# Gate stage of a PEER layer: eight tokens per set of tiles instead of four, two tokens innermost, and every low part of that stage on VectorE

## The chip, the core and the metric

The kernel runs on one core of one Trainium2 chip. The metric is the device time of one execution in microseconds (us); below, PE is TensorE, DVE is VectorE, ACT is ScalarE, POOL is GpSimd and SP the engine that issues the transfers from memory. PEld is TensorE's loading of stationary operands, which overlaps its matmuls.

## The reference, cut to what matters

Two blocks of a model are computed for 256 tokens of width 1024. The change lies in the PEER layer of the first block, which has 16384 experts, numbered by two indices of 128 each. Per token, 128 (expert, gate) pairs are selected:

```python
idx = jnp.take_along_axis(cidx, pos, axis=-1)      # cidx = i1 * 128 + i2
gates = jax.nn.softmax(best, axis=-1)
...
act = jax.nn.gelu(jnp.einsum('tkd,td->tk', ue, ht), approximate=False)
ve = jnp.take(v, it, axis=0)
return jnp.einsum('tk,tkd->td', gt * act, ve)
```

The kernel gathers nothing. It computes gelu(h · u) for all 16384 experts and all tokens, multiplies it by a gate that is zero for experts not selected, and multiplies by all of v.

## The kernel before, in words

**Units.** All weights stream through in units of 128x1024 fp32 (512 KB): SP loads unit i into `raw`, ACT writes its rounded high part `whi` (`hi`), and DVE or POOL writes the low part `wlo = raw - whi` (`lo`); `on_pool` decides which of the two by a table, and in the stretch `BASE["u"] + 62 <= slot <= BASE["v"] + 62` it gave every other unit to POOL. PE forms every product from three matmuls (high by high, high by low, low by high; `three`). There are three buffers of `whi` and `wlo`, so `hi` of unit i waits until PE is done with unit i - 3.

**Stages.** The 128 units of `u` are followed by the 128 units of `v`. A unit of u is 24 matmuls of 256 columns, a unit of v is 12 matmuls of 512 columns. ACT's gelu writes the activations `acts`, 128 partitions by 128 (second index) by 256 (tokens); in the views they are tile A. In the v stage ACT and DVE cut each slice of `acts` into a high part (`cut_acts`, into the buffer of hTh) and a low part (hTl), which PE then uses as stationary operands.

**The gate stage.** For each token PE makes the 128 x 64 gates of one half of the second index by three bf16 matmuls (the gate is split into three bf16 parts): stationary is a one-hot of the first index (`oh1`, tile oh), moving is a one-hot of the second index times the gate part (`og`). DVE builds these: `oh` by comparing `iota_b` with `row_b`, `og_eq` by comparing `iota_b` with `col_b`, `og` by multiplying `og_eq` with `gate3`. PE's product lands in a bank of PSUM and DVE multiplies it into `acts` (`weigh`; in the views "A<-A,bank"). Half 0 is done beside the units u+64 to u+127, half 1 beside v+0 to v+61; half 0 must be complete before v begins (ACT's `cut_acts` waits for `g_mul`), half 1 before v+64.

**What sets the order.** Each engine has its own program. After each unit a program calls `side.step()`, which advances the generator `gates(half)` to its next `yield`; `side.drain()` runs it to its end. Before the change one group is OB = 4 tokens, there are 64 groups a half, and one step is one group. DVE builds two groups ahead of what it weighs (two buffers each of `oh1` and `og`). A few steps are doubled (`U2_STEPS`, and n in (20, 40) in the v stage), so that the groups are done two units before the half's end. Before v+62 all programs call `side.drain()`.

Of the kernel before, what the change touches and what calls it, by code (L numbers as in the profile page):

```python
# [16 lines left out]
P = 128  # L17
D = 1024
T = 256
# [7 lines left out]
UNIT = 1024  # L27
NRAW = 4
NSPL = 3
OB = 4  # L30


STREAMS = [
# [80 lines left out]
def on_pool(i):  # L114

    slot = i - 2
    if BASE["u"] <= slot < BASE["u"] + 62:
        return True
    if BASE["u"] + 62 <= slot <= BASE["v"] + 62:
        return i % 2 == 1  # L120
    if BASE["w_xk"] <= slot < BASE["w_xk"] + 6 or BASE["w_up"] <= slot < BASE["w_up"] + 44:
        return i % 2 == 1
    return BASE["w2_t"] + 4 <= slot < BASE["w2_out"] + 8
# [12 lines left out]
UNITS = [(name, i) for name, k in STREAMS for i in range(k)]  # L136
ACC = {name: i + 1 for i, name in enumerate(("w_in_hi", "w_out", "v", "w_xv", "w2_out", "w_xo", "w_down"))}
U1_STEPS = (1,) * 13 + (2,)
U2_STEPS = (1,) * 31 + (2,)

SEMS = """
hi lo_dve lo_pool w acc0 ev_act ev_dve
# [47 lines left out]
def build(nc, x, mem, wdram, keep_d, con0_d, con1_d, con2_d, keys_d, w2c_d, gf_d, gf2_d, out):  # L190
    ctx = ExitStack()
    with ctx:
# [16 lines left out]
            iT = sb("iT", 3 * T, c=c)  # L209
        with ExitStack() as c:  # L210
            wgp = (sb("wgh", 8 * 36, F32R, c), sb("wgl", 8 * 36, F32R, c))
        oh1 = sb("oh1", 2 * OB * P, BF16)
        og_eq = sb("og_eq", OB * 64, BF16)
        og = sb("og", 2 * 3 * OB * 64, BF16)
        gate3 = sb("gate3", 3 * T, BF16)
        row_b = sb("row_b", T, BF16)
        col_b = sb("col_b", T, BF16)
        iota_b = sb("iota_b", P * OB, BF16)

        with ExitStack() as c:  # L220
            A1 = sb("A1", 24576, c=c)
# [21 lines left out]
        def t3(ap, a):  # L243
            return ap.rearrange("p (a b) -> p a b", a=a)
# [150 lines left out]
        def pe_program(e):  # L395
# [199 lines left out]
                yield  # L595

            def gates(half):
                for g in range(T // OB):
                    G = 64 * half + g
                    z = g % 2  # L600
                    o1 = t3(oh1[:, z * OB * P:(z + 1) * OB * P], P)
                    o3 = t4(og[:, z * 3 * OB * 64:(z + 1) * 3 * OB * 64], 3, 64)
                    if g:
                        yield
                    bk = 4 * half + g % 4
                    e.wait_ge(s["g_og"], G + 1)
                    use(bk)
                    for q in range(OB):
                        for j in range(3):
                            ins = mm(banks[bk][:, q * 64:(q + 1) * 64], o1[:, :, q], o3[:, j, :, q], j == 0, j == 2)  # L610
                    ins.then_inc(s["g_pe"], 1)
                    free[bk] = (s["g_mul"], G + 1)
                yield

            def mem_norm():
                for _ in range(4 + 2 + 2):
# [257 lines left out]
            side.drain()  # L874
            lin_T(BASE["u"] + 62, 2, hTv, KD)
            side.lists[0].append(gates(0))
            lin_T(BASE["u"] + 64, 64, hTv, KD, steps=U2_STEPS)
            side.drain()
            side.lists[0].append(gates(1))

# [2 lines left out]
            for n in range(128):  # L883
                if n == 62:
                    side.drain()
                if n == 126:
                    continue
                both = [n] if n < 126 else [126, 127]
                wv = [unit(BASE["v"] + m) for m in both]
                for m in both:  # L890
                    e.wait_ge(s["ca_lo"], m + 1)
                for b in range(TB):
                    for m, w in zip(both, wv):
                        for h in range(2):
                            ins = three(banks[2 * b + h][:, :], [z[:, m % 8, b * P:(b + 1) * P] for z in acth],
                                        [z[:, h * 512:(h + 1) * 512] for z in w], m == 0, m == 127)
                        if b == 1:
                            ins.then_inc(s["w"], 1)
                    if b == 0 and n == 127:
                        ins.then_inc(s["acc0"], 1)  # L900
                side.step(2 if n in (20, 40) else 1)
                if n == 72:
                    side.lists[0].append(mem_norm())
            for i in range(4):
# [67 lines left out]
        def act_program(e):  # L972
# [121 lines left out]
                for _ in range(8):  # L1094
                    yield

            def gates(half):
                for g in range(T // OB):
                    if g:
                        yield  # L1100
                yield

            def cut_acts(n):
                if n > 127:
                    return
                e.wait_ge(s["g_mul"], 64 if n < 64 else 128)
                e.wait_ge(s["w"], BASE["v"] + max(n - 7, 0))
                act(acth[0][:, n % 8, :], acts[:, n, :], ACT.Copy).then_inc(s["ca_hi"], 1)

# [226 lines left out]
            lin_T(BASE["u"], 62, gelu(0), steps=U1_STEPS)  # L1336
            side.drain()
            lin_T(BASE["u"] + 62, 2, gelu(62))
            side.lists[0].append(gates(0))
            lin_T(BASE["u"] + 64, 64, gelu(64), steps=U2_STEPS)  # L1340
            side.drain()
            side.lists[0].append(gates(1))
            cut_acts(0)
            cut_acts(1)
            for n in range(128):
                hi(BASE["v"] + n + 2)
                if n == 62:
                    side.drain()
                cut_acts(n + 2)
                if n == 126:  # L1350
                    continue
                side.step(2 if n in (20, 40) else 1)
                if n == 72:
                    side.lists[0].append(mem_norm())

# [82 lines left out]
        def dve_program(e):  # L1438
# [224 lines left out]
            def routing(b):  # L1663
# [43 lines left out]
                for _ in range(3):  # L1707
# [1 line left out]
                e.wait_ge(s["rt_pe"], b + 1)  # L1709
                e.tensor_copy(t3(iT[:, :], 3)[:, :, b * P:(b + 1) * P], t3(banks[b][:, 0:384], 3)  # L1710
                              ).then_inc(s["rt_dve"], 1)
                gt = iT[:, 2 * T + b * P:2 * T + (b + 1) * P]
                e.wait_ge(s["rt_dve"], 4 * b + 3)
                e.tensor_copy(row_b[:, b * P:(b + 1) * P], iT[:, b * P:(b + 1) * P])
                e.tensor_copy(col_b[:, b * P:(b + 1) * P], iT[:, T + b * P:T + (b + 1) * P])
                for j in range(3):
                    gj = gate3[:, j * T + b * P:j * T + (b + 1) * P]
                    if j < 2:
                        own(e.tensor_copy(gj, gt))
                        again()  # L1720
                        own(tt(gt, gt, gj, ALU.subtract))
                        again()
                    else:
                        e.tensor_copy(gj, gt).then_inc(s["rt_dve"], 1)
                yield

            def gates(half):
                lo64 = 64 * half
                e.wait_ge(s["rt_dve"], 8)

                def weigh(g):
                    G = 64 * half + g
                    t = g * OB
                    pb = banks[4 * half + g % 4]
                    e.wait_ge(s["ev_act"], PAIR_FREED[PAIR["u"] + 31 + 32 * half][1])
                    e.wait_ge(s["g_pe"], G + 1)
                    sl = acts[:, lo64:lo64 + 64, t:t + OB]
                    tt(sl, sl, pb[:, 0:64 * OB].rearrange("p (t i) -> p i t", t=OB), ALU.mult).then_inc(s["g_mul"], 1)

                for g in range(T // OB):  # L1740
                    G = 64 * half + g
                    z, t = g % 2, g * OB
                    o1 = oh1[:, z * OB * P:(z + 1) * OB * P]
                    o3 = og[:, z * 3 * OB * 64:(z + 1) * 3 * OB * 64]
                    if G >= 2:
                        e.wait_ge(s["g_pe"], G - 1)
                    shape = [P, P, OB]
                    tt(t3(o1, P), t3(iota_b[:, :], P), row_b[:, t:t + OB].unsqueeze(1).to_broadcast(shape),
                       ALU.is_equal)
                    shape = [P, 64, OB]  # L1750
                    if G:
                        e.wait_ge(s["g_og"], G)
                    own(tt(t3(og_eq[:, :], 64), t3(iota_b[:, lo64 * OB:(lo64 + 64) * OB], 64),
                           col_b[:, t:t + OB].unsqueeze(1).to_broadcast(shape), ALU.is_equal))
                    shape = [P, 3, 64, OB]
                    again()
                    tt(t4(o3, 3, 64), t3(og_eq[:, :], 64).unsqueeze(1).to_broadcast(shape),
                       t3(gate3[:, :], 3)[:, :, t:t + OB].unsqueeze(2).to_broadcast(shape), ALU.mult
                       ).then_inc(s["g_og"], 1)
                    if g:  # L1760
                        yield
                        weigh(g - 1)
                weigh(T // OB - 1)
                yield

            def cut_acts(n):
                if n > 127:
# [326 lines left out]
                norm_scale(1, xres, scr, b)  # L2094
            for k2 in range(4):
                norm_lo(1, "g_ffn", hTv, k2)
            own(e.tensor_copy(t3(iota_b[:, :], P), K_("iota").unsqueeze(2).to_broadcast([P, P, OB])))
            lin_T(BASE["w_pq"], 16)
            side.lists[0] += [routing(0), routing(1)]
            lin_T(BASE["u"], 62, steps=U1_STEPS)  # L2100
            side.drain()
            lin_T(BASE["u"] + 62, 2)
            side.lists[0].append(gates(0))
            lin_T(BASE["u"] + 64, 64, steps=U2_STEPS)
            side.drain()
            side.lists[0].append(gates(1))
            cut_acts(0)
# [1 line left out]
            for n in range(128):  # L2109
                lo(BASE["v"] + n + 2)  # L2110
                if n == 62:
                    side.drain()
                cut_acts(n + 2)
                if n == 126:
                    continue
                side.step(2 if n in (20, 40) else 1)
                if n == 72:
                    side.lists[0].append(mem_norm())

# [77 lines left out]
        def pool_program(e):  # L2197
# [49 lines left out]
            for n in range(128):  # L2247
                lo(BASE["v"] + n + 2)
                if n == 126:
                    continue  # L2250
                side.step(2 if n in (20, 40) else 1)
                if n == 72:
                    side.lists[0].append(mem_norm())
            rstd(3)
# [219 lines left out]
```

## Time and profile before

| | |
|---|---|
| median of three runs | 1638.8 us (1636.22 to 1640.73) |
| profiled execution, its own time | 1635.05 us |
| its span | 1633.3 us |
| mean granted clock of TensorE | 0.983 of full speed |
| units u+64 to u+127 with half 0 of the gates | about 483 to 717 us of the span |
| units v+0 to v+61 with half 1 of the gates | about 719 to 947 us |

The profiled execution's time is 1.75 us above its span. A time in a view counts from the span's start. A matmul's duration includes the way through the array, so the durations of neighbours overlap; what a matmul costs is the distance from its start to the next start.

### The profile page before, as it was taken

How to read it: one execution, taken by the hardware profiler on the slowest of the kernel's cores; microseconds unless marked ns; L12 is line 12 of the kernel's file. 1: busy time of each engine (PE TensorE's matmuls, PEld its weight loads, DVE VectorE, ACT ScalarE, POOL GpSimd, SP SyncE). 2: the span in 40 equal slices, each digit the busy share in tenths (PEclk: the TensorE clock that was granted, in tenths of full speed). 3: DMA queues.
4: the chain of work that ended last, by engine and by line, in shares of the span. 5: the costliest groups of instructions: out<-in, count | busy, mean ns of one | idle time of the engine just before them, and what ended most of it. 6: DMA issues, size and time to landing. Idle time of an engine off the chain costs nothing.

```text
span 1633.3 us, 26555 instructions
## 1 busy us (share of the span) xinstructions
PE 1521.8 (93%) x10784; PEld 1370.5 (84%) x10784; DVE 1142.6 (70%) x1894; ACT 719.4 (44%) x1031; POOL 488.5 (30%) x222
## 2 busy tenths in 40 slices
PE   7989989999999999999999999999886889898897
PEld 7979879989999999987777888888874668788876
DVE  4564653958838888879999966555689654577754
ACT  4762544444443333333333345445451544444443
POOL 4000000898963333333332300000353440133310
PEclk9999999999999999999999999999997899999999
DMA  6433454455554444444444466555322233444453
GB/s 219 132 127 106 142 175 160 164 161 180 168 181 143 142 143 140 146 134 151 141 144 142 142 237 215 183 191 168 130 95 73 82 128 113 142 155 155 155 183 114
DMA packets 66937, 245.15 MB, mean 150 GB/s; under 512 B 7424, under 2 KB 7552, under 8 KB 66560
## 3 DMA queue, kind: packets, MB, share of 16 engines
q1 hardware_dynamic: 66816, 243.45, 45.3%
q8 instruction: 86, 1.41, 0.4%
q14 instruction: 35, 0.29, 0.1%
HBM read 242.37 MB, written 1.05 MB: 149 GB/s over the span
## 4 chain that ended last, share of the span: by engine, by line
PE 70%; DVE 16%; ACT 7%; POOL 4%; issue 3%; DMA 0%; DVEq 0%; ACTq 0%; SPq 0%; POOLq 0%
PE bank L406 70%; DVE A L1448 4%; DVE A L1455 4%; ACT whi L978 4%; POOL wlo L2205 3%; DVE A L1452 2%; ACT A L978 2%; DVE wlo L1452 1%; PE bank L415 1%; DVE A L1449 1%; DVE A L1978 0%; ACT L978 0%; POOL small L2211 0%; DVE A L1991 0%; DVE xres L1452 0%
## 5 line engine op out<-in xcount | busy, mean ns | idle before, releaser
L978 ACT ACTIVATE whi<-raw 128x1024 fp32r<-128x1024 f32 x448 | 472.0, 1056 | 465.4 <-PE bank L406 464.0
L2205 POOL TENSOR_TENSOR wlo<-raw,whi 128x1024 fp32r<-128x1024 f32 x179 | 458.4, 2567 | 580.9 <-ACT whi L978 579.8
L406 PE MATMUL bank<-hTh,whi 128*128 128x256 f32 x1944 | 562.8, 290 | 30.2 <-DVE wlo L1452 16.4
L406 PE MATMUL bank<-hTh,wlo 128*128 128x256 f32 x1944 | 549.9, 283 | 0.0
L406 PE MATMUL bank<-hTl,whi 128*128 128x256 f32 x1944 | 549.5, 283 | 0.0
L1452 DVE TENSOR_TENSOR wlo<-raw,whi 128x1024 fp32r<-128x1024 f32 x269 | 329.2, 1226 | 274.6 <-ACT whi L978 274.1
L406 PEld LDWEIGHTS bank<-hTh,whi 128*128 128x128 f32 x1944 | 369.2, 190 | 40.2 <-DVE wlo L1452 23.4
L406 PEld LDWEIGHTS bank<-hTl,whi 128*128 128x128 f32 x1944 | 369.1, 190 | 0.8 <-issue 0.7
L406 PEld LDWEIGHTS bank<-hTh,wlo 128*128 128x128 f32 x1944 | 368.0, 189 | 0.0
L406 PE MATMUL bank<-whi,hTh 128*128 128x512 f32 (+2 forms) x560 | 223.8, 400 | 5.7 <-POOL wlo L2205 2.3
L406 PE MATMUL bank<-whi,hTl 128*128 128x512 f32 (+2 forms) x560 | 218.6, 390 | 0.0
L406 PE MATMUL bank<-wlo,hTh 128*128 128x512 f32 (+2 forms) x560 | 217.7, 389 | 0.0
L978 ACT ACTIVATE A<-bank 128x512 f32<-128x512 f32 (+2 forms) x169 | 91.3, 553 | 232.1 <-PE bank L406 226.2
L2211 POOL TENSOR_TENSOR small<-small 128x1 f32<-128x1 f32 x16 | 8.8, 551 | 550.2 <-DVE small L1449 550.2
L406 PEld LDWEIGHTS bank<-whi,hTh 128*128 128x128 f32 x560 | 106.7, 191 | 28.3 <-issue 4.5
L406 PEld LDWEIGHTS bank<-whi,hTl 128*128 128x128 f32 x560 | 105.5, 188 | 24.0
L406 PEld LDWEIGHTS bank<-wlo,hTh 128*128 128x128 f32 x560 | 105.9, 189 | 21.5
L1452 DVE TENSOR_TENSOR hTl<-A,hTh 128x256 fp32r<-128x256 f32 x128 | 111.6, 873 | 17.2 <-ACT hTh L978 17.1
L406 PE MATMUL bank<-og,oh 128*128 128x64 bf16 x1536 | 116.5, 241 | 2.6 <-DVE og L1452 2.6
L406 PEld LDWEIGHTS bank<-og,oh 128*128 128x128 bf16 x1536 | 93.8, 119 | 23.7 <-issue 16.2
L406 PE MATMUL bank<-A 128*128 128x128 f32 (+9 forms) x528 | 87.4, 325 | 24.4 <-DVE A L1452 21.6
L406 PEld LDWEIGHTS bank<-A 128*128 128x128 f32 (+4 forms) x528 | 70.3, 192 | 35.5 <-DVE A L1452 13.9
(143 smaller groups left out, 1624.7 us busy)
## 6 DMA issues: line engine op xcount, KB each, us to landing
raw<-in_u SPq DMA_DIRECT2D x128, 512.0 KB, 3.3
raw<-in_v SPq DMA_DIRECT2D x128, 512.0 KB, 3.3
raw<-in_w_up SPq DMA_DIRECT2D x44, 512.0 KB, 3.3
raw<-in_w_down SPq DMA_DIRECT2D x22, 512.0 KB, 3.3
raw<-in_w_in_t SPq DMA_DIRECT2D x18, 512.0 KB, 3.5
raw<-in_w_in_g SPq DMA_DIRECT2D x16, 512.0 KB, 3.4
raw<-in_w_out SPq DMA_DIRECT2D x16, 512.0 KB, 3.3
raw<-in_w_pq SPq DMA_DIRECT2D x16, 512.0 KB, 3.3
```

The costliest lines, as they stand in the source:

```text
L406: return e.matmul(o, l, r, start=st, stop=sp_, skip_group_check=True)
L415: return e.transpose(o, i, ident[0:k, 0:k])
L978: return e.activation(o, i, func, **kw)
L1448: return e.tensor_scalar(o, i, s1, None, op0)
L1449: return e.tensor_scalar(o, i, s1, s2, op0, op1)
L1452: return e.tensor_tensor(o, a, b, op)
L1455: return e.scalar_tensor_tensor(o, a, z, b, op0, op1)
L2205: e.tensor_tensor(l, raw[i % NRAW][:, :], h.bitcast(F32), ALU.subtract).then_inc(s["lo_pool"], 1)
L2211: e.tensor_tensor(st[:, 2:3], st[:, 3:4], mhalf, ALU.pow).then_inc(s["n_rstd"], 1)
```

## The change

A group becomes eight tokens (OB = 8), so 32 groups a half. `oh1` and `og` are single buffers of the same total size, laid out with two tokens innermost (pair of tokens, then index, then token within the pair), where four tokens were innermost. Each group takes two steps: DVE weighs the group before and builds the next in the first, PE multiplies in the second. The doubled steps are gone. `on_pool` no longer gives POOL any unit of the gate stage.

```diff
-OB = 4
+OB = 8
+OP = OB // 2
...
-    if BASE["u"] + 62 <= slot <= BASE["v"] + 62:
-        return i % 2 == 1
...
-        oh1 = sb("oh1", 2 * OB * P, BF16)
+        oh1 = sb("oh1", OB * P, BF16)
         og_eq = sb("og_eq", OB * 64, BF16)
-        og = sb("og", 2 * 3 * OB * 64, BF16)
+        og = sb("og", 3 * OB * 64, BF16)
...
-        iota_b = sb("iota_b", P * OB, BF16)
+        iota_b = sb("iota_b", P * 2, BF16)
...
             def gates(half):
+                o1 = t4(oh1[:, :], OP, P)
+                o3 = og[:, :].rearrange("p (m j i r) -> p m j i r", m=OP, j=3, r=2)
                 for g in range(T // OB):
-                    G = 64 * half + g
-                    z = g % 2
-                    o1 = t3(oh1[:, z * OB * P:(z + 1) * OB * P], P)
-                    o3 = t4(og[:, z * 3 * OB * 64:(z + 1) * 3 * OB * 64], 3, 64)
-                    if g:
-                        yield
+                    G = 32 * half + g
                     bk = 4 * half + g % 4
+                    yield
                     e.wait_ge(s["g_og"], G + 1)
                     use(bk)
                     for q in range(OB):
                         for j in range(3):
-                            ins = mm(banks[bk][:, q * 64:(q + 1) * 64], o1[:, :, q], o3[:, j, :, q], j == 0, j == 2)
+                            ins = mm(banks[bk][:, q * 64:(q + 1) * 64], o1[:, q // 2, :, q % 2], o3[:, q // 2, j, :, q % 2],
+                                     j == 0, j == 2)
                     ins.then_inc(s["g_pe"], 1)
                     free[bk] = (s["g_mul"], G + 1)
-                yield
+                    yield
...
-            lin_T(BASE["u"] + 64, 64, hTv, KD, steps=U2_STEPS)
+            lin_T(BASE["u"] + 64, 64, hTv, KD)
...
-                side.step(2 if n in (20, 40) else 1)
+                side.step()
...
+                def build(g):
+                    G, t = 32 * half + g, g * OB
+                    if G:
+                        e.wait_ge(s["g_pe"], G)
+                    rows, cols_ = (z[:, t:t + OB].rearrange("p (m r) -> p m r", r=2) for z in (row_b, col_b))
+                    shape = [P, OP, P, 2]
+                    tt(o1, io.unsqueeze(1).to_broadcast(shape), rows.unsqueeze(2).to_broadcast(shape), ALU.is_equal)
+                    shape = [P, OP, 64, 2]
+                    if G:
+                        e.wait_ge(s["g_og"], G)
+                    own(tt(eq, io[:, lo64:lo64 + 64, :].unsqueeze(1).to_broadcast(shape),
+                           cols_.unsqueeze(2).to_broadcast(shape), ALU.is_equal))
+                    shape = [P, OP, 3, 64, 2]
+                    again()
+                    tt(o3, eq.unsqueeze(2).to_broadcast(shape),
+                       gv[:, t // 2:t // 2 + OP, :, :].unsqueeze(3).to_broadcast(shape), ALU.mult).then_inc(s["g_og"], 1)
...
                 for g in range(T // OB):
...
                     if g:
-                        yield
                         weigh(g - 1)
+                    build(g)
+                    yield
+                    yield
                 weigh(T // OB - 1)
-                yield
```

Beside this, `gate3` is written by `routing` in the new layout, and the waits for `g_mul` count 32 and 64 where they counted 64 and 128.

On DVE, in the u half, one low part was followed by a set of four gate instructions twice over (the other unit's low part was POOL's). One such set, before, with the semaphores that each row waits for:

```order
L1452 TENSOR_TENSOR wlo<-raw,whi 128x1024 [waits s_hi]
L1452 TENSOR_TENSOR A<-A,bank 128x64x4 [waits s_g_pe,s_ev_act]
L1452 TENSOR_TENSOR oh<-iota_b,row_b 128x512 [waits s_g_pe]
L1452 TENSOR_TENSOR og_eq<-iota_b,col_b 128x256 [waits s_g_og]
L1452 TENSOR_TENSOR og<-og_eq,gate 128x768 [waits s_own_dve]
```

The same place after the change:

```order
L1440 TENSOR_TENSOR wlo<-raw,whi 128x1024 [waits s_hi] x2
L1440 TENSOR_TENSOR A<-A,bank 128x64x8 [waits s_g_pe,s_ev_act]
L1440 TENSOR_TENSOR oh<-iota_b,row_b 128x1024 [waits s_g_pe]
L1440 TENSOR_TENSOR og_eq<-iota_b,col_b 128x512 [waits s_g_og]
L1440 TENSOR_TENSOR og<-og_eq,gate 128x1536 [waits s_own_dve]
```

Two units now share one set of four instructions of twice the size, and DVE has both low parts.

On DVE at the end of half 1, before unit v+62, hTl is the low part of a slice of `acts`. Before the change:

```order
L1452 TENSOR_TENSOR og<-og_eq,gate 128x768 [waits s_own_dve]
L1452 TENSOR_TENSOR hTl<-A,hTh 128x256 [waits s_ca_hi]
L1452 TENSOR_TENSOR A<-A,bank 128x64x4 [waits s_g_pe,s_ev_act] x2
L1452 TENSOR_TENSOR wlo<-raw,whi 128x1024 [waits s_hi]
L1452 TENSOR_TENSOR hTl<-A,hTh 128x256 [waits s_ca_hi]
```

After it:

```order
L1440 TENSOR_TENSOR wlo<-raw,whi 128x1024 [waits s_hi]
L1440 TENSOR_TENSOR hTl<-A,hTh 128x256 [waits s_ca_hi]
L1440 TENSOR_TENSOR wlo<-raw,whi 128x1024 [waits s_hi]
L1440 TENSOR_TENSOR A<-A,bank 128x64x8 [waits s_g_pe,s_ev_act]
L1440 TENSOR_TENSOR oh<-iota_b,row_b 128x1024 [waits s_g_pe]
L1440 TENSOR_TENSOR og_eq<-iota_b,col_b 128x512 [waits s_g_og]
L1440 TENSOR_TENSOR og<-og_eq,gate 128x1536 [waits s_own_dve]
L1440 TENSOR_TENSOR A<-A,bank 128x64x8 [waits s_g_pe,s_ev_act]
L1440 TENSOR_TENSOR hTl<-A,hTh 128x256 [waits s_ca_hi]
```

The second low part is that of unit v+64; the last group is now built behind it, where the last group before was built ahead of the last two weighings.

On PE at the same place, before the change, the last group and unit v+62:

```order
L406 MATMUL bank<-whi,hTl 128x512
L406 MATMUL bank<-og,oh 128x64 [waits s_g_mul,s_g_og]
L406 MATMUL bank<-og,oh 128x64 x11
L406 MATMUL bank<-whi,hTh 128x512 [waits s_ca_lo,s_lo_dve]
L406 MATMUL bank<-wlo,hTh 128x512
```

After it:

```order
L404 MATMUL bank<-whi,hTl 128x512
L404 MATMUL bank<-og,oh 128x64 [waits s_g_mul,s_g_og]
L404 MATMUL bank<-og,oh 128x64 x23
L404 MATMUL bank<-og,oh 128x64 [waits s_g_mul,s_g_og]
L404 MATMUL bank<-og,oh 128x64 x23
L404 MATMUL bank<-whi,hTh 128x512 [waits s_ca_lo,s_lo_dve]
```

The last two groups now stand directly behind one another, with no unit between them; everywhere else a group of 24 follows every second unit.

## Rows read from the trace of the kernel before

**Rows 1.** The page: busy time of each engine; chain that ended last; gate matmuls.

```profile
PE 1521.8 (93%) x10784; PEld 1370.5 (84%) x10784; DVE 1142.6 (70%) x1894; ACT 719.4 (44%) x1031; POOL 488.5 (30%) x222
...
PE 70%; DVE 16%; ACT 7%; POOL 4%; issue 3%; DMA 0%; DVEq 0%; ACTq 0%; SPq 0%; POOLq 0%
...
L406 PE MATMUL bank<-og,oh 128*128 128x64 bf16 x1536 | 116.5, 241 | 2.6 <-DVE og L1452 2.6
```

**Rows 2.** Windows, the two halves: busy us (instructions) by engine; granted clock; DMA.

```profile
483.00:717.00 234.00, 232.92 (x2280) 229.56 (x2280) 197.62 (x286) 81.61 (x94) 82.39 (x32) 1.00 0.44 143
...
719.00:947.00 228.00, 226.84 (x1517) 180.77 (x1517) 212.67 (x350) 85.44 (x126) 74.49 (x31) 1.00 0.45 147
```

**Rows 3.** Waits, 483 to 950 us: us in total, times, longest.

```profile
PE bank L406 <- DVE og L1452: 2.6, 6, 1.2
PE bank L406 <- DVE hTl L1452: 1.5, 1, 1.5
```

**Rows 4.** Timeline of PE, first two groups: start, duration, [idle before <-releaser].

```profile
483.77 0.92 PE L406 MATMUL bank<-og,oh 128*128 128x64 bf16 x12 [1.15 <-DVE og L1452]
...
487.33 0.28 PE L406 MATMUL bank<-hTh,wlo 128*128 128x256 f32 x1
487.46 0.92 PE L406 MATMUL bank<-og,oh 128*128 128x64 bf16 x12
...
488.39 0.28 PE L406 MATMUL bank<-hTl,whi 128*128 128x256 f32 x1
```

**Rows 5.** Timeline of PE at a doubled step of the u half.

```profile
571.96 0.27 PE L406 MATMUL bank<-hTh,wlo 128*128 128x256 f32 x1
572.08 1.74 PE L406 MATMUL bank<-og,oh 128*128 128x64 bf16 x24
...
573.82 0.28 PE L406 MATMUL bank<-hTl,whi 128*128 128x256 f32 x1
573.94 0.28 PE L406 MATMUL bank<-hTh,wlo 128*128 128x256 f32 x1
```

**Rows 6.** Timeline of DVE in the u half: one low part and its gate instructions.

```profile
489.23 1.23 DVE L1452 TENSOR_TENSOR wlo<-raw,whi 128x1024 fp32r<-128x1024 f32 x1 [0.74 <-ACT whi L978]
490.38 0.41 DVE L1452 TENSOR_TENSOR A<-A,bank 128x256 f32<-128x256 f32 x1
490.71 0.41 DVE L1452 TENSOR_TENSOR oh<-iota_b,row_b 128x512 bf16<-128x512 bf16 x1
491.04 0.28 DVE L1452 TENSOR_TENSOR og_eq<-iota_b,col_b 128x256 bf16<-128x256 bf16 x1
491.36 0.56 DVE L1452 TENSOR_TENSOR og<-og_eq,gate 128x768 bf16<-128x768 bf16 x1
...
492.84 2.48 DVE L1452 TENSOR_TENSOR og_eq<-iota_b,col_b 128x256 bf16<-128x256 bf16 x1
```

**Rows 7.** Timeline of all engines at the last group of half 1.

```profile
945.24 0.92 PE L406 MATMUL bank<-og,oh 128*128 128x64 bf16 x12
...
945.50 1.06 ACT L978 ACTIVATE whi<-raw 128x1024 fp32r<-128x1024 f32 x1 [2.24 <-PE bank L406]
...
946.26 0.42 DVE L1452 TENSOR_TENSOR A<-A,bank 128x256 f32<-128x256 f32 x1 [0.22 <-PE bank L406]
```

**Rows 8.** Timeline of all engines between u and v.

```profile
716.92 0.28 PE L406 MATMUL bank<-hTh,wlo 128*128 128x256 f32 x1
...
717.73 0.71 ACT L978 ACTIVATE hTh<-A 128x256 fp32r<-128x256 f32 x2
...
718.17 0.76 DVE L1452 TENSOR_TENSOR hTl<-A,hTh 128x256 fp32r<-128x256 f32 x2 [4.70 <-ACT hTh L978]
...
718.74 0.48 PE L406 MATMUL bank<-whi,hTh 128*128 128x512 f32 x1 [1.54 <-DVE hTl L1452]
```

**Rows 9.** Windows of a later stage, around an idle stretch of PE.

```profile
1339.84:1343.26 3.42, 1.00 (x9) 0.82 (x8) 1.81 (x5) 3.17 (x9) 0.00 (x0) 1.00 0.70 235
1343.26:1346.67 3.41, 3.41 (x18) 3.41 (x17) 2.55 (x5) 1.29 (x2) 0.00 (x0) 0.50 0.02 5
1346.67:1350.08 3.41, 3.41 (x31) 3.41 (x30) 1.23 (x1) 1.14 (x2) 0.00 (x0) 1.00 0.45 154
```

More of the change, by code:

```diff
@@ L138 @@
 U1_STEPS = (1,) * 13 + (2,)
-U2_STEPS = (1,) * 31 + (2,)
 SEMS = """
@@ L1095, in routing @@
                     yield
-            def gates(half):
-                for g in range(T // OB):
-                    if g:
-                        yield
-                yield
             def cut_acts(n):
@@ L1105, in cut_acts @@
                     return
-                e.wait_ge(s["g_mul"], 64 if n < 64 else 128)
+                e.wait_ge(s["g_mul"], 32 if n < 64 else 64)
                 e.wait_ge(s["w"], BASE["v"] + max(n - 7, 0))
@@ L1338, in act_program @@
             lin_T(BASE["u"] + 62, 2, gelu(62))
[L1339 to L1342, printed above, removed]
+            lin_T(BASE["u"] + 64, 64, gelu(64))
             cut_acts(0)
@@ L1351, in act_program @@
                     continue
-                side.step(2 if n in (20, 40) else 1)
+                side.step()
                 if n == 72:
@@ L1711, in routing @@
                               ).then_inc(s["rt_dve"], 1)
-                gt = iT[:, 2 * T + b * P:2 * T + (b + 1) * P]
+                gt = t3(iT[:, 2 * T + b * P:2 * T + (b + 1) * P], 64)
                 e.wait_ge(s["rt_dve"], 4 * b + 3)
@@ L1716, in routing @@
                 for j in range(3):
-                    gj = gate3[:, j * T + b * P:j * T + (b + 1) * P]
+                    gj = gate3[:, :].rearrange("p (m j r) -> p m j r", j=3, r=2)[:, 64 * b:64 * b + 64, j, :]
                     if j < 2:
@@ L1729, in gates @@
                 e.wait_ge(s["rt_dve"], 8)
+                o1, o3 = t4(oh1[:, :], OP, P), og[:, :].rearrange("p (m j i r) -> p m j i r", m=OP, j=3, r=2)
+                eq, io = t4(og_eq[:, :], OP, 64), t3(iota_b[:, :], P)
+                gv = gate3[:, :].rearrange("p (m j r) -> p m j r", j=3, r=2)
+                def build(g):
[14 more added lines that the diff above has]
+                       gv[:, t // 2:t // 2 + OP, :, :].unsqueeze(3).to_broadcast(shape), ALU.mult).then_inc(s["g_og"], 1)
                 def weigh(g):
-                    G = 64 * half + g
-                    t = g * OB
-                    pb = banks[4 * half + g % 4]
+                    G, t = 32 * half + g, g * OB
                     e.wait_ge(s["ev_act"], PAIR_FREED[PAIR["u"] + 31 + 32 * half][1])
@@ L1737, in weigh @@
                     sl = acts[:, lo64:lo64 + 64, t:t + OB]
-                    tt(sl, sl, pb[:, 0:64 * OB].rearrange("p (t i) -> p i t", t=OB), ALU.mult).then_inc(s["g_mul"], 1)
+                    tt(sl, sl, banks[4 * half + g % 4][:, :].rearrange("p (t i) -> p i t", t=OB), ALU.mult
+                       ).then_inc(s["g_mul"], 1)
                 for g in range(T // OB):
[L1741 to L1759, printed above, removed]
                     if g:
-                        yield
                         weigh(g - 1)
+                    build(g)
+                    yield
+                    yield
                 weigh(T // OB - 1)
-                yield
             def cut_acts(n):
@@ L2096, in dve_program @@
                 norm_lo(1, "g_ffn", hTv, k2)
-            own(e.tensor_copy(t3(iota_b[:, :], P), K_("iota").unsqueeze(2).to_broadcast([P, P, OB])))
+            own(e.tensor_copy(t3(iota_b[:, :], P), K_("iota").unsqueeze(2).to_broadcast([P, P, 2])))
             lin_T(BASE["w_pq"], 16)
@@ L2103, in dve_program @@
             side.lists[0].append(gates(0))
-            lin_T(BASE["u"] + 64, 64, steps=U2_STEPS)
+            lin_T(BASE["u"] + 64, 64)
             side.drain()
@@ L2115, in dve_program @@
                     continue
-                side.step(2 if n in (20, 40) else 1)
+                side.step()
                 if n == 72:
@@ L2250, in pool_program @@
                     continue
-                side.step(2 if n in (20, 40) else 1)
+                side.step()
                 if n == 72:
```

## Prediction

> **What bounds the kernel now.** I read the page first: PE is busy 93% of the span, and it holds 70% of the chain that ended last, so a microsecond counts only if PE stands still less or does less [rows 1]. Then the two halves of the gate stage by themselves: PE is busy 232.9 of 234 us and 226.8 of 228 us, at full clock, while DVE has 198 and 213 us, its waits for POOL included, and POOL 82 and 74 [rows 2]. PE's waits there are few: 2.6 us in six waits for DVE's `og`, and 1.5 us once for the first low part of `acts` between u and v [rows 3]. What frees DVE or POOL has nothing else to give back. The timelines then show how PE pays for the gates [rows 4, 5], how long DVE's pieces take [rows 6], and the two places where the halves end [rows 7, 8].
>
> **Fewer groups on PE: a gain of 4.3 us.** The 1536 gate matmuls stay 1536 [rows 1]. From the last matmul ahead of a group to the second behind it 1.06 us pass (487.33 to 488.39), where two matmuls without a group take 2 x 0.12 [rows 4, 5]; a group of 12 thus costs 0.82 us. Its matmuls start (0.92 - 0.24)/11 = 0.0616 us apart, 0.242 being the mean duration of one [rows 1, 4]; twelve make 0.74. The rest, 0.07 to 0.08, is the change from fp32 to bf16 matmuls and back. The x24 row is the check: the second dozen behind the first adds 1.74 - 0.92 = 0.82 to the row with a wait of some 0.1 inside, and no second change [rows 5]. I take 0.07 per group, in both halves. Before there are 128 groups, four of them directly behind another by the doubled steps, so PE changes over 124 times; afterwards 63 times. 61 x 0.07 = 4.3 us. Should a merged group save nothing, that is 0; the x24 row speaks against it.
>
> **Waits that go: 3.6 us.** The idle time of a wait counts from the end of the matmul before, which lies 0.28 - 0.12 = 0.16 us behind the moment when the next would have started [rows 4, 5]. So the six waits cost 2.6 + 6 x 0.16 = 3.6 us; the first, at 483.77, alone 1.3. They stand at the first group of a half, where PE asks in the step in which DVE begins to build, and at the doubled steps. Afterwards PE asks one unit later than DVE builds, and no step is doubled.
>
> **Is DVE in time everywhere else?** Take the start of a group on PE as zero. The unit ahead is then done, so ACT's `hi` starts at 0.26 and takes 1.06 [rows 7]; DVE's low part follows and holds DVE for 1.15 (489.23 to 490.38) [rows 6], to 2.47. `weigh` held it for 0.33 with 256 elements per partition [rows 6]; twice as many cost 0.27 more, at the roughly one element per ns that the 1024 of a low part need: to 3.07. The build, from `oh`'s start to `og`'s end, took 1.21 (490.71 to 491.92); every 256 elements more cost 0.14 (`og_eq` with 256 in 0.28, `oh` with 512 in 0.41, `og` with 768 in 0.56), so the doubled one takes 1.21 + 6 x 0.14 = 2.05 and ends at 5.1 [rows 6]. In the v half the low part of `acts` comes in between, 0.34 (two take 0.76, the first 0.42) [rows 8]: 5.5. PE asks at twice 234/64 or 228/62, some 7.2 with the merged groups [rows 2]. So it is hidden with 1.7 us to spare. POOL's low parts cost DVE the wait inside the 2.48 us of an `og_eq` that otherwise takes 0.28 [rows 6]; this 2.2 us per pair of units goes, one low part of 1.15 comes, and both lie under PE: nothing.
>
> **Two tokens innermost.** The trace before shows rows of four elements, not of two. From below nothing changes; from above an element takes a full cycle, 0.28 per 256 in place of 0.14: build 1.21 - 6 x 0.14 + 12 x 0.28 = 3.7. That ends at 7.1, just in time, and shows only where the build is exposed, at v+62: 1.7 us. I take the lower end, since rows of four ran at two elements a cycle without a gap between rows [rows 6]. The Trainium skill, "VectorE: DVE Perf Modes", section "What auto-detection actually checks", has two elements a cycle for 16-bit tensors with a step of one and says nothing of row length. By that rule the sum stands as below; by the slower end it is 1.7 us worse. No row here shows such a short row.
>
> **Between u and v: a loss of 0.25 us.** Before, the last group was done two units early, and PE stood from 716.92 to 718.74, 1.82 - 0.12 = 1.7 us lost [rows 8]. Now a group of 24 ends the half. `weigh` started 1.02 behind the start of a group of 12 (945.24 to 946.26) [rows 7], so 1.02 + 0.74 = 1.76 behind one of 24, and takes 0.42 + 0.27; ACT's cut begins at 2.5, DVE's part 0.44 later, PE 0.57 after that [rows 8]: 3.5. PE itself is busy for 1.55 of it, so 1.95 are lost in place of 1.7.
>
> **At v+62: a loss of 3.65 us, and the clock.** Here PE drains: groups 30 and 31 stand one behind the other. Group 31 is built behind the low part of v+64, which waits for `hi`, which waits for unit v+61. By the times above the build ends at 5.1 and PE, free at 1.5, starts at 5.15. Behind it wait unit v+62 and all that follows; before, nothing waited here. Of a stretch with PE idle for 2.4 of 3.4 us the trace shows what comes next: 3.41 us at clock 0.50, that is 1.2 in place of 2.4 GHz, with 18 matmuls in place of 31 [rows 9], a loss of 13/31 x 3.41 = 1.4 us. After the 1.54 us of idle time between u and v the clock stayed at 1.00 [rows 2, 8]. 3.5 us is nearer to the former: I add 1.4, and 0 is the bound below. Between u and v, at 1.8 us idle, I add none; 1.4 is the bound there.
>
> **Sum.** -4.3 - 3.6 + 0.25 + 3.65 + 1.4 = -2.6 us against the profiled execution's own 1635.05, its span of 1633.3 and 1.75 around it: 1632.5. That execution lies 3.75 us below the median of the runs; on the median of 1638.8 the sum gives 1636.2. Its own bounds are -4.0 (the clock holds) and +0.5 (one element a cycle, and the clock falls between u and v too), 1634.8 and 1639.3; should the merges save nothing on top of that, 1643.6.
>
> **Rivals.** *The gate matmuls get faster.* Both operands were read with a step of 8 bytes and now of 4. 64 columns at the fp32 pace of 256 in 0.12 us would take 0.03, and the matmuls start 0.0616 apart [rows 4, 5]; if the step sets that, up to 0.031 x 1536 = 47 us are to be had, and if the loading of 128 stationary columns sets it, nothing. I take nothing, for in the u half the loads are as dense as the matmuls, 229.6 and 232.9 of 234 us [rows 2]; a third of it would be 15 us, time 1621. The Trainium skill, "Advanced Engine Details and Errata", section "SBUF Cachelines", says that two accesses to one 16-byte line already give full speed. By that rule 8 bytes were enough and this rival is worth 0; no run here shows a smaller step.
>
> *DVE becomes the bound.* If rows of two elements cost more than a cycle per element, the build no longer ends by 7.2: from 3.7 us on it decides. At three cycles per row it takes some 5.5: late by 1.7 us for 31 groups in v and 1.35 for 32 in u, 96 us, so about 1732. For it speaks that DVE now has one set of buffers and nothing built ahead; against it the rows of four without a gap.
>
> *PE waits elsewhere* because the single `oh` and `og` let DVE build nothing until PE has read the group before: a late low part then delays the next group too. With 0.3 us for each of 63 groups that is 19 us, 1655. The spare 1.7 us speaks against it.
>
> **How the numbers follow.** A run of this kernel tells some 0.3%, 4.9 us, from no change. The forecast has a chance of 0.62, of which 0.10 lies below 1633.9, as the runs shown scatter by 2 us to either side; faster matmuls 0.20; DVE as the bound 0.07; other waits 0.11, one of these small enough to be no change (0.03). Faster 0.30, same 0.55, slower 0.15. The range for 8 in 10 is 1621 to 1642: the forecast's own 1634.8 to 1639.3 with some 2.5 us of scatter above, and the faster matmuls down to a third of what the step could give.
>
> **What would show it.** Right: gate groups as x24 rows of some 1.65 us, 0.0616 from start to start; PE's waits for `og` down to one of 3 to 3.5 us near 940 us, followed by a stretch at clock 0.5; `oh`, `og_eq`, `og` at about 0.70, 0.42 and 0.98 us; no POOL between u+64 and v+62. Wrong: gate matmuls closer than 0.06; `og` over 1.8 us and a PE wait at every group; no wait near 940.

## Result, and the profile after

The changed kernel takes 1591.08 us (median of four runs, 1587.08 to 1593.47) beside 1637.51 for the kernel before in the same comparison: ratio 0.9716, 95% interval 0.9685 to 0.9746. It is 46 us faster; the forecast was 1636.2, and the range ended at 1621.

The page of the changed kernel: busy time by engine, the chain that ended last, and the loads of the stationary operands of the gate matmuls.

```profile
PE 1475.5 (93%) x10784; PEld 1331.6 (84%) x10784; DVE 1058.9 (67%) x1702; ACT 719.5 (45%) x1031; POOL 329.5 (21%) x158
...
PE 71%; DVE 15%; ACT 7%; POOL 4%; issue 2%; DMA 0%; DVEq 0%; SPq 0%; ACTq 0%; POOLq 0%
...
L404 PEld LDWEIGHTS bank<-og,oh 128*128 128x128 bf16 x1536 | 50.5, 98 | 14.5 <-issue 8.5
```

PE's instructions are as many as before, yet it is busy 46.3 us less, and it still holds the chain [rows 1]: work on the bounding engine became shorter. The group of gate matmuls in the gate stage says which (busy us, mean ns of one, idle before):

```profile
L404 PE MATMUL bank<-og,oh 128*128 128x64 bf16 x1536 | 58.2, 194 | 4.3 <-DVE og L1440 4.3
```

The same 1536 matmuls had 116.5 us [rows 1]. The timeline of PE shows their pace, in u and at the end of half 1:

```profile
565.59 0.90 PE L404 MATMUL bank<-og,oh 128*128 128x64 bf16 x24
572.16 0.90 PE L404 MATMUL bank<-og,oh 128*128 128x64 bf16 x24
...
885.72 0.90 PE L404 MATMUL bank<-og,oh 128*128 128x64 bf16 x24
892.16 0.90 PE L404 MATMUL bank<-og,oh 128*128 128x64 bf16 x24
897.32 1.46 PE L404 MATMUL bank<-og,oh 128*128 128x64 bf16 x24 [4.25 <-DVE og L1440]
898.60 0.78 PE L404 MATMUL bank<-whi,hTh 128*128 128x512 f32 x1
```

A row marked x24 is 24 matmuls in a run, and its duration reaches from the first start to the last end: 0.90 us. Less the 0.194 of the last matmul that is 23 steps of 0.0307 us. Before, a step was 0.0616 [rows 4]. 1536 x 0.0309 = 47.5 us. A group with its two units now takes 6.57 us in u and 6.44 in v. Everything else is smaller. PE's waits in the gate stage (us in total, times, longest):

```profile
PE bank L404 <- DVE og L1440: 4.3, 1, 4.3
PE bank L404 <- DVE hTl L1440: 1.9, 1, 1.9
```

The six short waits for `og` [rows 3] have gone and one has come. The windows around it show the clock (busy us by engine; granted clock, DMA share, GB/s at the end):

```profile
896.00:897.00 1.00, 0.00 (x0) 0.00 (x0) 0.97 (x2) 0.00 (x0) 0.00 (x0) 0.92 1.01 410
897.00:898.00 1.00, 0.68 (x13) 0.68 (x14) 0.26 (x1) 0.00 (x0) 0.00 (x0) 0.50 0.83 332
...
899.00:900.00 1.00, 1.00 (x3) 0.74 (x3) 0.58 (x1) 0.39 (x1) 0.00 (x0) 0.50 0.00 0
900.00:901.00 1.00, 1.00 (x5) 0.84 (x4) 0.43 (x1) 0.03 (x1) 0.00 (x0) 0.88 0.00 0
```

At 0.5 from just before 897.0 to about 900.2, with PE at work from 897.32: some 2.9 us at half speed, a loss of 1.5. And DVE's instructions in the gate stage:

```profile
L1440 DVE TENSOR_TENSOR og<-og_eq,gate 128x1536 bf16<-128x1536 bf16 x64 | 61.3, 958 | 2.2
L1440 DVE TENSOR_TENSOR oh<-iota_b,row_b 128x1024 bf16<-128x1024 bf16 x64 | 43.8, 685 | 0.0
L1440 DVE TENSOR_TENSOR A<-A,bank 128x512 f32<-128x512 f32 x64 | 43.6, 681 | 2.5 <-PE bank L404 2.5
...
L1440 DVE TENSOR_TENSOR og_eq<-iota_b,col_b 128x512 bf16<-128x512 bf16 x64 | 26.8, 419 | 0.0
```

Rows of two elements run at the pace that rows of four had [rows 6].

### The profile page after: what moved, and what is told of

The parts are those of the page before. It is cut to its first block, busy times and chain, and to the rows that moved or that the text cites. A ratio compares the mean times of both kernels' runs of the same rounds, so it can differ in the third digit from the quotient of the medians.

```text
span 1588.7 us, 26171 instructions
## 1 busy us (share of the span) xinstructions
PE 1475.5 (93%) x10784; PEld 1331.6 (84%) x10784; DVE 1058.9 (67%) x1702; ACT 719.5 (45%) x1031; POOL 329.5 (21%) x158
## 3 DMA queue, kind: packets, MB, share of 16 engines
HBM read 242.37 MB, written 1.05 MB: 153 GB/s over the span
## 4 chain that ended last, share of the span: by engine, by line
PE 71%; DVE 15%; ACT 7%; POOL 4%; issue 2%; DMA 0%; DVEq 0%; SPq 0%; ACTq 0%; POOLq 0%
PE bank L404 70%; DVE A L1436 4%; DVE A L1443 4%; ACT whi L975 4%; POOL wlo L2194 3%; DVE A L1440 3%; ACT A L975 2%; DVE wlo L1440 1%; PE bank L413 1%; DVE A L1437 1%; ACT L975 1%; DVE A L1967 0%; POOL small L2200 0%; DVE A L1980 0%; DVE xres L1440 0%
## 5 line engine op out<-in xcount | busy, mean ns | idle before, releaser
L1440 DVE TENSOR_TENSOR wlo<-raw,whi 128x1024 fp32r<-128x1024 f32 x333 | 407.2, 1225 | 336.2 <-ACT whi L975 335.7
L2194 POOL TENSOR_TENSOR wlo<-raw,whi 128x1024 fp32r<-128x1024 f32 x115 | 298.2, 2602 | 273.0 <-ACT whi L975 272.0
L1440 DVE TENSOR_TENSOR A<-A,bank 128x512 f32<-128x512 f32 (+1 forms) x109 | 65.3, 599 | 7.3 <-PE bank L404 6.3
L1440 DVE TENSOR_TENSOR og<-og_eq,gate 128x1536 bf16<-128x1536 bf16 x64 | 61.3, 958 | 2.2
L404 PEld LDWEIGHTS bank<-og,oh 128*128 128x128 bf16 x1536 | 50.5, 98 | 14.5 <-issue 8.5
```

Of the source, the lines that this page charges most:

```text
L404: return e.matmul(o, l, r, start=st, stop=sp_, skip_group_check=True)
L1440: return e.tensor_tensor(o, a, b, op)
L2194: e.tensor_tensor(l, raw[i % NRAW][:, :], h.bitcast(F32), ALU.subtract).then_inc(s["lo_pool"], 1)
```

## Experiments

The theory after the result: the distance in bytes from one column of an operand to the next sets the pace of the gate matmuls, 8 before, 4 now. The rivals: the groups of eight or the move of the low parts made the gain, or PE was held up by something that only looks like pace. No experiment leaves out any part of the computation.

**step_alone.** The kernel before, groups of four and POOL as they were, only two tokens innermost (DVE's views and `gate3` to match):

```diff
-o1 = t3(oh1[:, z * OB * P:(z + 1) * OB * P], P)
-o3 = t4(og[:, z * 3 * OB * 64:(z + 1) * 3 * OB * 64], 3, 64)
+o1 = t4(oh1[:, z * OB * P:(z + 1) * OB * P], OP, P)
+o3 = og[:, ...].rearrange("p (m j i r) -> p m j i r", m=OP, j=3, r=2)
```

> The kernel before (groups of four tokens, two sets of tiles, doubled steps, every other low part of the gate stage on POOL), with one thing taken from the change: two tokens innermost in oh and og, so that TensorE reads both operands with a step of 4 bytes in place of 8. Theory 'step': the gate matmuls start 0.031 us apart in place of 0.061, 1536 of them save 47 us, so about 1591 us (0.971 of before). Rival 'grouping': the pace comes from the longer rows of 24 matmuls or from POOL's absence; then it stays at 0.061 and 1637 us.

Measured: 1606.59 us, ratio 0.9809 (0.9770 to 0.9848). The pace came, but some 16 us of the gain stayed out. A row of 12 gate matmuls:

```profile
570.68 0.55 PE L407 MATMUL bank<-og,oh 128*128 128x64 bf16 x12
```

(0.55 - 0.194)/11 = 0.032 us apart. PE's waits, then a piece of DVE's timeline in v, then what POOL does meanwhile:

```profile
PE bank L407 <- DVE og L1454: 15.5, 17, 1.2
```

```profile
701.54 2.50 DVE L1454 TENSOR_TENSOR hTl<-A,hTh 128x256 fp32r<-128x256 f32 x1
703.96 0.41 DVE L1454 TENSOR_TENSOR A<-A,bank 128x256 f32<-128x256 f32 x1
...
706.55 0.42 DVE L1454 TENSOR_TENSOR hTl<-A,hTh 128x256 fp32r<-128x256 f32 x1
...
708.58 2.43 DVE L1454 TENSOR_TENSOR hTl<-A,hTh 128x256 fp32r<-128x256 f32 x1
```

```profile
701.28 2.47 POOL L2208 TENSOR_TENSOR wlo<-raw,whi 128x1024 fp32r<-128x1024 f32 x1 [5.10 <-ACT whi L980]
```

The same `hTl` takes 0.42 us alone and 2.50 beside POOL's low part, and ends 0.29 us behind it. (The Trainium skill, "SBUF — State Buffer", section "SBUF: two separate sides", has a GpSimd instruction that reads SBUF and a VectorE instruction with two inputs in SBUF share a pair of ports, which the one that starts first holds for its whole instruction. The trace agrees: this `hTl`, with both inputs in SBUF, started 0.26 us behind POOL's row.) DVE so needs 7.04 us for two units and their groups (701.54 to 708.58), where the changed kernel's PE asks every 6.44. The waits are 15.5 us in place of 2.6, eleven more of them at 0.16 each [rows 4, 5]: 14.7 of the 16 us.

**four_innermost.** The changed kernel with four tokens innermost again (8 bytes), groups of eight and the low parts left as changed; `RS` tokens stand innermost in `oh1`, `RM` in `og`:

```diff
-OP = OB // 2
+RS, RM = 4, 4
...
-mm(banks[bk][:, q * 64:(q + 1) * 64], o1[:, q // 2, :, q % 2], o3[:, q // 2, j, :, q % 2],
+mm(banks[bk][:, q * 64:(q + 1) * 64], o1[:, q // RS, :, q % RS], o3[:, q // RM, j, :, q % RM],
```

> The changed kernel (eight tokens a group, one set of tiles, no low parts on POOL), with four tokens innermost again, so a step of 8 bytes. Theory 'step': matmuls 0.061 us apart, rows of 24 of some 1.65 us, and the time of the prediction's own sum, -2.6 us on the time before: 1635 (0.998), with a wait of 3.6 us before v+62. Rival 'grouping': 0.031 apart and 1591.

Measured: 1635.09 us, ratio 0.9987 (0.9965 to 1.0009, ten runs). Its timeline and its waits:

```profile
566.60 1.66 PE L406 MATMUL bank<-og,oh 128*128 128x64 bf16 x24
573.91 1.66 PE L406 MATMUL bank<-og,oh 128*128 128x64 bf16 x24
```

```profile
PE bank L406 <- DVE og L1442: 3.5, 1, 3.5
PE bank L406 <- DVE hTl L1442: 1.9, 1, 1.9
```

23 steps of 0.0617 us, and two units with their group take 7.31 us where the changed kernel takes 6.57. That is 0.74 per group, 64 x 0.74 = 47 us. This kernel is what the forecast described (a row of 1.66 us, one wait of 3.5), and the change without its step is within the noise.

**step_oh_only** and **step_og_only.** The same edit with `RS, RM = 2, 4` (the stationary `oh1` at 4 bytes, the moving `og` at 8), and with `RS, RM = 4, 2`.

> The changed kernel with two tokens innermost in oh alone (stationary operand, step 4 bytes) and four in og (moving operand, step 8 bytes). Theory 'moving': the moving operand's step sets the pace, so 0.061 us apart and about 1635. Rival 'loading': the stationary operand's step does, so 0.031 and 1591.

> The changed kernel with two tokens innermost in og alone (moving operand, step 4 bytes) and four in oh (stationary operand, step 8 bytes). Theory 'moving': 0.031 us apart and about 1591. Rival 'loading': 0.061 and 1635. If both this run and the one with oh alone stay at 0.061, both operands count, each by itself enough to hold the pace down.

Measured: 1631.49 and 1592.71 us (one run each, so the pace in the timeline counts here more than the times). A row of 24 from each, first the stationary alone, then the moving alone:

```profile
562.10 1.63 PE L406 MATMUL bank<-og,oh 128*128 128x64 bf16 x24
```

```profile
563.73 0.97 PE L406 MATMUL bank<-og,oh 128*128 128x64 bf16 x24
```

(1.63 - 0.241)/23 = 0.0604 and (0.97 - 0.198)/23 = 0.0336. The moving operand sets the pace; the stationary one adds 0.001 to 0.003 us.

**moving_2_bytes** and **moving_16_bytes.** `RS, RM = 2, 1` and `RS, RM = 2, 8`: is it the bytes spanned, or one threshold?

> The changed kernel with one token innermost in og, so that the moving operand is read without a gap (2 bytes from column to column); oh1 stays at 4 bytes; nothing of the computation is left out. If PE takes the bytes that the moving operand spans at 8.3 a ns, a gate matmul goes from 0.031 to 0.015 us, or to the time that its weights take if that is longer. If what counts is one access for each pair of 4 bytes, or another floor, it stays at 0.027 to 0.031. DVE's og and og_eq have rows of one element innermost from stride-0 operands and may double, so the time may be higher, 1590 to 1640, and is not the point.

> The changed kernel with eight tokens innermost in og (16 bytes from column to column), oh1 at 4 bytes; nothing of the computation is left out. If the time goes with the bytes that the columns span, a gate matmul takes 0.122 us and the kernel 1591 + 1536 x 0.092 = 1732, less what PE's waits give back, 1725 to 1735. If a step over 4 bytes costs half the pace once and no more, 0.061 us and 1630 to 1637.

Measured: 1592.88 and 1742.86 us (one run each). The row of 24 at 2 bytes, and DVE's `og` there, with rows of one element:

```profile
564.14 0.88 PE L406 MATMUL bank<-og,oh 128*128 128x64 bf16 x24
```

```profile
L1442 DVE TENSOR_TENSOR og<-og_eq,gate 128x1536 bf16<-128x1536 bf16 x64 | 112.5, 1758 | 2.2
```

The row of 24 at 16 bytes, and a window of u with its granted clock (0.96):

```profile
563.62 2.96 PE L406 MATMUL bank<-og,oh 128*128 128x64 bf16 x24
```

```profile
566.00:610.00 44.00, 44.00 (x360) 43.77 (x359) 24.91 (x31) 13.02 (x15) 0.00 (x0) 0.96 0.34 119
```

At 16 bytes the step from start to start is 0.1158 us, near twice that at 8; at 2 bytes it is 0.0298, hardly better than at 4. So at the 4, 8 and 16 bytes tried the pace goes with the bytes spanned (8.3 to 8.8 bytes per ns and partition), and from 4 to 2 bytes it stays at a floor of 0.03 us for 64 columns. 2 bytes give PE nothing, and cost DVE 0.8 us per `og`. The 16-byte kernel is 21 us slower than its pace explains (1591 + 1536 x 0.085 = 1722); the granted clock, in this stage of the changed kernel 1.00 but for the stretch behind 897 us, was 0.89 to 0.98 in seven windows from 480 to 1045 us, although PE stood still for only 2 us of them. What these windows lost by the clock adds up to some 28 us, more than enough for the 21; the row above is not touched by it (clock 1.00 from 560 to 580 us). Why the clock fell with PE at work is open.

**low_parts_on_pool.** The changed kernel with the lines of the low parts put back:

```diff
+    if BASE["u"] + 62 <= slot <= BASE["v"] + 62:
+        return i % 2 == 1
```

> This is the changed kernel with every second low part of the gate stage back on POOL; nothing of the computation is left out. Theory: since a gate matmul of 64 columns now takes 0.031 us, PE needs only some 6.45 us for two units and their group of eight in the first half of v, and DVE is close behind it. With POOL at work beside it, DVE's own group lasts longer (in the run of the step alone the og_eq row was 0.92 us in place of 0.33), so DVE needs some 6.7 us and PE waits for og: some 8 us over the gate stage, a time near 1599, and the row of PE's waits for og at 8 us or more. Rival: the low parts' place is free, as I predicted: 1591, og wait 4.3.

Measured: 1598.13 us, ratio 0.9759 (0.9718 to 0.9801), and as waits:

```profile
PE bank L406 <- DVE og L1442: 9.9, 4, 4.9
```

7 us more than the changed kernel's median, though the intervals of the two ratios overlap. The waits are the firmer sign: 5.6 us more of them, three of 1.7 us in v and one of 4.9 at its end; in u there is none.

**fours_no_pool.** step_alone with these two lines taken out: groups of four in two sets of tiles, no POOL.

> The kernel before with two innermost and all low parts of the gate stage on DVE, but still groups of four in two sets of tiles; nothing of the computation is left out. If POOL beside DVE is what cost the step alone its 15.5 us of waits for og, they go: DVE needs some 6.1 us for two units and two groups of four, PE some 6.5. Time 1591 to 1594 (62 change-overs more than the changed kernel, some 4 us, but no single wait of 4.3 us after the first half). If the groups of eight are what counts, the waits stay at 12 us or more and the time at 1603 to 1607.

Measured: 1591.64 us, ratio 0.9713 (0.9679 to 0.9746), with PE's waits:

```profile
PE bank L405 <- DVE og L1452: 4.1, 6, 1.2
PE bank L405 <- DVE hTl L1452: 1.5, 1, 1.5
```

Taking POOL out gives step_alone the missing 15 us, and the groups of eight then add nothing to the median. That is a balance, as two groups of four in v show:

```profile
711.58 0.54 PE L405 MATMUL bank<-og,oh 128*128 128x64 bf16 x12
714.85 0.54 PE L405 MATMUL bank<-og,oh 128*128 128x64 bf16 x12
```

Two units with their two groups take 2 x 3.27 = 6.54 us, with one group of eight 6.44; in u it is 6.68 and 6.57. The 0.1 per pair of units is some 6 us in both halves, and the 4.1 us of waits for `og` go too. Against that the groups of eight have the wait of 4.3 us at v+62 and the slow clock behind it. (Its profiled execution, at 1600.17 us the longest of its five, lost time at a clock of 0.87 between 200 and 240 us, before the gate stage.)

**group_earlier**, with **after_again**, the changed kernel unaltered on the same chip. What the groups of eight cost, the wait at v+62, is removed by building the first groups earlier; of DVE's lines (PE's list is begun sooner in the same way):

```diff
+side.lists[0].append(gates(0))
 lin_T(BASE["u"] + 62, 2)
-side.lists[0].append(gates(0))
...
+side.step()
 for n in range(128):
+    if n < 62:
+        side.step()
     lo(BASE["v"] + n + 2)
...
-    side.step()
+    if n >= 62:
+        side.step()
```

> The changed kernel with the first group of each half built earlier, so that PE needs nothing of DVE at once: in u the list of groups is begun two units sooner, in v one step is taken before the first unit, and for the first 62 units of v DVE takes its step ahead of the low part, not behind it. Nothing of the computation is left out. If the one wait of 4.3 us for og after the first half of v, and the clock that falls to 0.5 behind it (1.4 us), are what the groups of eight cost, the wait falls below 1 us and the time by 5 to 6 us, to some 1585 (0.996 of the changed kernel). Rival: the wait only moves (DVE's work is the same, and PE gets to the end of u sooner), and the time stays at 1589 to 1592.

> The changed kernel unaltered, to be compared on the same chip with the one whose first groups come earlier: 1591, one og wait of 4.3 us near 897.

Measured: 1582.52 us (five runs), ratio to the kernel before 0.9666 (0.9644 to 0.9689), against 1590.39 and 0.9712 (0.9688 to 0.9736) for the changed kernel beside it. The waits for `og` are gone; all that is left in the gate stage is the wait between u and v, and PE works through the v half (702 to 905 us) at full clock:

```profile
PE bank L404 <- DVE hTl L1441: 1.5, 1, 1.5
...
702.00:905.00 203.00, 203.00 (x1484) 162.47 (x1483) 170.05 (x246) 87.43 (x128) 0.00 (x0) 1.00 0.55 172
```

7.9 us between the medians. Of these 4.3 are the wait and 0.3 the shorter wait for `hTl`; the clock behind the wait comes on top. How much that is differs between executions of the same kernel: in after_again it stayed at 0.5 until 903.5, with PE at work throughout:

```profile
898.20:905.00 6.80, 6.80 (x29) 5.46 (x27) 1.11 (x2) 1.45 (x3) 0.00 (x0) 0.61 0.01 4
905.00:925.00 20.00, 20.00 (x87) 16.08 (x86) 11.18 (x15) 9.90 (x16) 0.00 (x0) 1.00 0.57 192
```

6.2 us at half speed, a loss of 3.1 in place of 1.5. With 1.5 to 3.1 the sum is 6.1 to 7.7, and what is left of the 7.9 is within the scatter of the runs. This is the fastest version measured here.

## Why the prediction was wrong

**The step that failed: "I take nothing" in the rival *The gate matmuls get faster*.** The forecast left a gate matmul at 0.0616 us; it took 0.0307, and the runs show that the 8 bytes between the columns of the moving operand had held it there (four_innermost, step_oh_only, step_og_only). The rival had the mechanism, the place and the price (47 us as the upper bound), with a chance of 0.20. Two arguments stood against it. That the loads are as dense as the matmuls [rows 2] holds for either cause, since every matmul here has its load; step_oh_only and step_og_only show that the load was not it. And the section "SBUF Cachelines" of the Trainium skill's "Advanced Engine Details and Errata" has two accesses to a 16-byte line at full speed; the moving operand with 8 bytes from column to column ran at 0.0604 to 0.0617 us per 64 columns and with 4 at 0.031, so for this operand the measurement decides against that rule. The row that pointed the right way was the fp32 pace: 256 columns, 4 bytes apart, in 0.12 us, thus 64 in 0.03 [rows 4]. It is just what came. The range went wrong at the same place: it ended at a third of the rival's price, for which there was no row; its bounds were 0 and 47.

**The rest of the sum.** Four_innermost is its test: forecast -2.6 us, measured a ratio of 0.9987, that is -2.1 us (-5.7 to +1.5). "Waits that go" went, and "At v+62" has its wait of 3.5 (3.65 with the 0.16 of [rows 4, 5]). In the changed kernel the second group there starts 5.16 us behind the first (forecast 5.15), but PE is done with the first 0.75 us sooner, so the wait is 4.25; the clock took 1.5 for 1.4, which is in part luck, since it took 3.1 in after_again. "Two tokens innermost" had 0.70, 0.42 and 0.98 us for `oh`, `og_eq` and `og`, measured 0.685, 0.419 and 0.958. The terms "Fewer groups on PE" (4.3) and "Between u and v" (0.25; its wait rose by 0.4) are below what the times can tell, but the traces have the first: two units with two groups of four take 7.36 us in u and 7.23 in v before, and 7.31 and 7.18 with one group of eight in four_innermost. A merged pair so saved 0.05 us, not 0.07, and all of them some 3.1.

**A step right for the wrong pace: "nothing" for POOL's low parts.** It fits a PE that asks every 7.2 us. With 6.44 in v, DVE's spare time per pair of units is 0.88 us in place of 1.7, as its idle time ahead of a low part in the changed kernel shows:

```profile
893.51 1.22 DVE L1440 TENSOR_TENSOR wlo<-raw,whi 128x1024 fp32r<-128x1024 f32 x1 [0.88 <-ACT whi L975]
```

By the prediction's own numbers POOL's low part costs DVE 2.2 - 1.15 = 1.05 us more per pair than doing it itself, which is less than 1.7 and more than 0.88. So POOL's low parts cost some 7 us with groups of eight (low_parts_on_pool) and 15 with groups of four (step_alone against fours_no_pool). The rival in which DVE becomes the bound was there, but tied to slow rows of two, which did not come; a faster PE has the same effect.

**The account.** -47.5 for the pace, -2.6, +0.8 for the longer wait: -49.3. With 3.1 for the merged groups, 0.4 more between u and v and 1.5 for the clock it is -47.6. The medians give -46.4, and the interval of the ratio -41.6 to -51.6. Nothing is left over that can be told from noise. Of the parts of the change, the step alone gave 30 us; the low parts made the other 15 available; the groups of eight gave nothing in the median, because the wait at v+62 takes back what they save. Without that wait (group_earlier) the ratio is 0.9666 beside the 0.9713 of fours_no_pool, some 8 us; the two intervals just overlap.

Left open: why the pace has this form (bytes spanned, a floor at 4) is not settled by these runs; steps between 4 and 8 bytes were not tried. Whether the floor belongs to the columns or to the loads is not shown either. For the columns speaks that the fp32 matmuls, with one load for 256 columns, take the same 0.12/256 us a column [rows 4]; for the loads, that the step went from 0.0307 to 0.0336 us when `oh1` alone was changed.

## What to carry to other kernels

Look at the distance in bytes between the columns of a moving operand, not only at its element type: where several items stand innermost for DVE's sake, two bf16 were enough to keep DVE at its pace, and more slowed PE in proportion. When the bounding engine gets faster, work out anew the spare time of every engine called hidden, with the new interval between its requests. Where two bounds of a cost lie 47 us apart and only an argument lies between them, keep both in the range.

## What the runs showed of the hardware that was not expected

- The moving operand of a 64-column bf16 matmul: 0.0298, 0.0307, 0.0604 and 0.1158 us from start to start at 2, 4, 8 and 16 bytes from column to column, with the stationary operand at 4 bytes. The stationary operand at 8 bytes lengthened the pace by 0.003 us at most. A load took 98 ns on average with both operands at 4 bytes, and 115 to 118 where either was at 8: the load's duration followed the moving operand too, and did not set the pace.
- DVE's `og` took 958 ns with rows of two elements and 1758 with rows of one, at the same 1536 elements.
- A low part on POOL stretched the DVE instruction that started during it, here a `hTl` from 0.42 to 2.50 us beside a POOL instruction of 2.47. In the gate stage of step_alone this fell on instructions with both inputs in SBUF; the 128 `A<-A,bank`, one input of which is in PSUM, took 0.41 to 0.42 us throughout.
- After the same idle time of 4.25 us the clock stayed at half speed for some 3.4 us in one execution and 6.8 in another. In the 16-byte kernel it was below full speed (0.96 from 566 to 610 us) with PE never idle there.
